# Four RMS norms moved into the stages that produce their input, and two plain fp32 slices at the start of three output projections

## The reference, cut to what matters

```python
def rms_norm(x, g):
    xf = x.astype(jnp.float32)
    y = xf * lax.rsqrt(jnp.mean(xf * xf, axis=-1, keepdims=True) + EPS)
    return (y * g.astype(jnp.float32)).astype(x.dtype)

x = x + jnp.concatenate([y_a, y_b, y_m], axis=-1) @ w_out   # even layer; the odd layer has the same form
```

## Time and profile before

| | |
|---|---|
| median of 3 runs | 2514.02 us (2512.58 to 2516.36) |
| the profiled execution's own time | 2516.36 us |
| its span on the core | 2515.1 us |
| PE busy | 2372.6 us (94%) |
| DVE busy | 1924.6 us (77%) |
| ACT busy | 1162.9 us (46%) |
| mean granted TensorE clock | 0.971 of full speed |
| `even_out` | 194 to 232 us |
| `odd_out` | 430 to 470 us |
| LRU block | 480 to 582 us |
| `mla_out` | 1584 to 1618 us |

### The profile page before, as it was taken

One profiled execution on the slowest core, in us unless ns is written; L12 is line 12 of the kernel. 1 busy time (PEld: TensorE's weight loads), 2 busy tenths in 40 slices (PEclk: granted clock), 3 DMA queues, 4 the chain that ended last, 5 costly groups with the idle time before them and its releaser, 6 DMA issues. The chain is left out here.

```text
span 2515.1 us, 37964 instructions
## 1 busy us (share of the span) xinstructions
PE 2372.6 (94%) x11691; PEld 1939.4 (77%) x11691; DVE 1924.6 (77%) x4365; ACT 1162.9 (46%) x2015; POOL 153.2 (6%) x170
## 2 busy tenths in 40 slices
PE   7998989898998999999999989899899999999997
PEld 5775457675886888888888856678778888888886
DVE  5676677765998788888888855589977777777776
ACT  5674245341177544444444434414854444444443
POOL 0000000000253000000000000013500000000000
PEclk9998988998999999999999989899999999999999
DMA  7523640564112676777767751212055555555553
GB/s 259 186 89 127 232 169 1 179 231 143 59 51 71 209 254 251 261 255 247 257 249 259 257 182 68 84 59 85 26 177 195 188 189 194 185 195 188 191 193 134
DMA packets 144614, 429.30 MB, mean 171 GB/s; under 512 B 15231, under 2 KB 21375, under 8 KB 144511
## 3 DMA queue, kind: packets, MB, share of 16 engines
q1 hardware_dynamic: 144510, 428.08, 48.7%
HBM read 426.99 MB, written 1.05 MB: 170 GB/s over the span
## 5 line engine op out<-in xcount | busy, mean ns | idle before, releaser
L3241 PE MATMUL bank<-h_t_parts,u_t_high 128*128 128x512 f32 x1824 | 450.5, 389 | 0.0
L3241 PEld LDWEIGHTS bank<-h_t_parts,u_t_high 128*128 128x128 f32 x1824 | 342.5, 188 | 71.0
L3325 ACT ACTIVATE u_t_high<-u_ring 128x1024 fp32r<-128x1024 f32 x228 | 242.0, 1061 | 184.3 <-DMA u_ring<-in_peer_u 182.3
L3344 ACT ACTIVATE activated<-activated 128x256 f32<-128x256 f32 x228 | 95.7, 420 | 472.5 <-DVE activated L3394 472.5
L3255 PE MATMUL bank<-v_high,weighted_high 128*128 128x512 f32 x976 | 306.2, 395 | 5.4 <-DVE weighted_low L3406 5.4
L3381 DVE TENSOR_TENSOR u_t_low<-u_ring,u_t_high 128x1024 fp32r<-128x1024 f32 x228 | 278.8, 1223 | 40.5 <-ACT u_t_high L3325 28.9
L3255 PE MATMUL bank<-v_low,weighted_high 128*128 128x512 f32 x976 | 303.9, 392 | 0.0
L3255 PE MATMUL bank<-v_high,weighted_low 128*128 128x512 f32 x976 | 302.5, 391 | 0.0
L3388 DVE TENSOR_TENSOR v_low<-v_ring,v_high 128x1024 fp32r<-128x1024 f32 x244 | 296.9, 1217 | 6.0 <-ACT v_high L3332 3.3
L3332 ACT ACTIVATE v_high<-v_ring 128x1024 fp32r<-128x1024 f32 x244 | 257.1, 1054 | 49.6 <-PE bank L3255 48.1
L3244 PEld LDWEIGHTS bank<-h_t_parts,u_t_low 128*128 128x128 f32 x1824 | 248.9, 190 | 17.7
(11 more groups left out here) (588 smaller groups left out, 3682.1 us busy)
## 6 DMA issues: line engine op xcount, KB each, us to landing
v_ring<-in_peer_v SPq DMA_DIRECT2D x244, 512.0 KB, 3.4
u_ring<-in_peer_u SPq DMA_DIRECT2D x228, 512.0 KB, 4.6
panel<-in_l_w_in SPq DMA_DIRECT2D x15, 2048.0 KB, 8.0
late_tiles<-in_ada_w SPq DMA_DIRECT2D x54, 512.0 KB, 4.3
mod_ring<-in_ada_w SPq DMA_DIRECT2D x42, 512.0 KB, 4.6
panel<-in_peer_w_q SPq DMA_DIRECT2D x8, 2048.0 KB, 7.8
panel<-in_l_w_out SPq DMA_DIRECT2D x4, 2560.0 KB, 8.9
early_u<-in_peer_u SPq DMA_DIRECT2D x20, 512.0 KB, 3.4
```

The source lines that it names most:

```text
L3241: nc.tensor.matmul(banks[2 + k][:, :], UTH[:, k, j, :], H2[:, j, :, :].rearrange("p a s -> p (a s)"), start=(j == 0), stop=False, skip_gro ...
L3325: nc.scalar.activation(UTH[:, s, :, :].rearrange("p a b -> p (a b)"), UR[:, s, :], ACT.Copy)\
L3344: nc.scalar.activation(AA[:, s, :], AA[:, s, :], ACT.Gelu).then_inc(gelued, 1)
```

## The change

It touches nothing but the four places and what lies between them.

- `project_rows` takes `plain=2`: the first two slices of the first panel are one plain fp32 product per row tile, of the panel as it was loaded and a plain fp32 copy `SP` of the turned source (ACT, into a tile of its own). Their weights are not split in panel 0. `SH` of these slices is still made by ACT in turn, `SL` by DVE from `SP` and `SH` behind `w_low` of the last slice of panel 0, since panel 1 needs them.
- Three turns come first, and `turn(m + 3)` stands behind slice m, instead of two and `turn(m + 2)`.
- `half_squares`: the norm's squares are summed by halves of 512 columns as `X` is finished: ACT does (panel 0, both row tiles) behind `w_high` of slice 5 of panel 1 and (panel 1, row tile 0) at the end, each into a PSUM bank that nobody reads; DVE does (panel 1, row tile 1), and adds the two sums.
- The rest of the norm (`normed_turned`, unchanged) follows in the same stage, in the three projections and in the LRU block. Four norm stages go.
- The two gain stages become `gain_work`, DVE work ahead of the last results in `odd_out` and in the LRU block. Two stages go.

```diff
@@ project_rows @@
+        xn = nc.alloc_sbuf_tensor_at(f"rows_normed{n}", [P, NT, D], F32, offset=zone.at)
...
+        x_done = [sem(f"rows{n}_x_done{x}") for x in range(4)]
+        squares_act, squares_dve = half_squares([banks[4], banks[5]])
+        end_act, end_dve, end_pe = normed_turned(X, xn, jobs)
...
+        SP = zone("plain_rows", [P, plain, S]) if plain else None
...
             def _(pe):
                 def turn(m):
-                    if m >= 4:
-                        pe.wait_ge(src_low, m - 3)
+                    if m - 4 >= plain:
+                        pe.wait_ge(src_low, m - 3 - plain)
+                    elif m >= 4:
+                        pe.wait_ge(src_high, m - 3)
...
-                turn(0)
-                turn(1)
+                for m in range(3):
+                    turn(m)
...
-                    if i == 0:
-                        pe.wait_ge(src_low, m + 1)
-                    pe.wait_ge(w_low, q + 1)
-                    high, low = ring[:, q % 4, 0, :], ring[:, q % 4, 1, :]
+                    if q < plain:
+                        pe.wait_ge(src_plain, m + 1)
+                        if m == 0:
+                            wait_panel(pe, ps[i])
+                        products = ((SP, weights(q)),)
+                    else:
+                        n = nth[q]
+                        if i == 0:
+                            pe.wait_ge(src_low, m + 1 - plain)
+                        elif i == 1 and m < plain:
+                            pe.wait_ge(src_low, K - plain + m + 1)
+                        pe.wait_ge(w_low, n + 1)
+                        high, low = ring[:, n % 4, 0, :], ring[:, n % 4, 1, :]
+                        products = ((SH, high), (SH, low), (SL, high))
...
-                    if i == 0 and m + 2 < K:
-                        turn(m + 2)
+                    if i == 0 and m + 3 < K:
+                        turn(m + 3)
+                end_pe(pe)
...
             def _(act):
...
                     if i == 0:
                         act.wait_ge(turned, m + 1)
+                        if m < plain:
+                            nc.scalar.activation(SP[:, m, :], banks[4 + m % 4][:, 0:S], ACT.Copy).then_inc(src_plain, 1)
                         nc.scalar.activation(SH[:, m, :], banks[4 + m % 4][:, 0:S], ACT.Copy).then_inc(src_high, 1)
...
+                    if i == 1 and m == 5:
+                        for t in range(NT):
+                            x_there(act, 0, t)
+                            squares_act(f, act, 0, t)
                 sqrt_table()
+                x_there(act, 1, 0)
+                squares_act(f, act, 1, 0)
+                end_act(f, act)
...
             def _(dve):
...
+                    if i == 0 and m == K - 1:
+                        for x in range(plain):
+                            nc.vector.tensor_tensor(SL[:, x, :], SP[:, x, :], SH[:, x, :].bitcast(F32), ALU.subtract)\
+                                .then_inc(src_low, 1)
                     if m == 2 and i > 0:
                         evacuate(f, dve, i - 1)
                     modulation.add(f, dve, plan[q])
+                if gains:
+                    gains(f)
                 evacuate(f, dve, len(ps) - 1)
+                x_there(dve, 1, 1)
+                squares_dve(f, dve, xn[:, 1, 512:1024])
+                end_dve(f, dve)
@@ new @@
+    def half_squares(junk):
+        sq = sem(f"norm{Stage.count}_half_squares")
+        cell = lambda i, t: stats[:, 60 + 2 * i + t:61 + 2 * i + t]
+        half = lambda i, t: X[:, t, i * 512:(i + 1) * 512]
+
+        def on_act(f, act, i, t):
+            if i:
+                act.wait_ge(sq, t + 1)
+            f(nc.scalar.activation(junk[t][:, :], half(i, t), ACT.Square, accum_out=cell(i, t)), sq, wait=False)
+
+        def on_dve(f, dve, own):
+            f(nc.vector.scalar_tensor_tensor(own, half(1, 1), 1.0, half(1, 1), ALU.mult, ALU.mult, accum_out=cell(1, 1)))
+            dve.wait_ge(sq, 3)
+            f(nc.vector.tensor_tensor(stats[:, 0:2], stats[:, 60:62], stats[:, 62:64], ALU.add))
+        return on_act, on_dve
@@ lru_block, on DVE @@
+                gain_work([(1, sc2, C("norm_ffn_g_2", 0, 8))], 24, 40)(f)
                 dve.wait_ge(row_stored, 2)
...
+                squares_dve(f, dve, xn[:, 1, 512:1024])
+                end_dve(f, dve)
@@ callers @@
-    norm_transpose(X, HT, [(HT, C("l1_norm", 0, 8), None)])
...
-    gain_stage([(0, sc1, C("norm_mix_g_2", 0, 8))], 0, 16)
-    norm_transpose(X, HT, [(HT, GM[:, 0, :], sh1)])
...
-    def peer(l, q_name, gain, shift, gate_cols, jobs=None, gains=None):
-        norm_transpose(X, HT, [(HT, gain, shift)])
+    def peer(l, q_name, gate_cols, jobs=None, gains=None):
...
-    gain_stage([(1, sc2, C("norm_ffn_g_2", 0, 8))], 24, 40)
```

More of the change, by code:

```diff
@@ L521, in project_split, with project_rows @@
         zone.at = mark
-    def project_rows(name, rows, order, evac, ready=None, at_act=None, at_dve=None, at_pe=None, mod_steps=(0, 0)):
+    def project_rows(name, rows, order, evac, jobs, gains=None, gated=False, ready=None, at_act=None, at_dve=None,
+                     at_pe=None, mod_steps=(0, 0), plain=0):
         if not stage():
@@ L546, in weights, with wait_used @@
             return slots[ps[i] % 3][:, order[m] * 512:(order[m] + 1) * 512]
-        def wait_used(eng, q):
-            i, m = slices[q]
+        split_of = slices[plain:]
+        nth = {q: q - plain for q in range(plain, len(slices))}
+        def wait_used(eng, n):
+            i, m = split_of[n]
             if m == K - 1:
@@ L558, in evacuate, with x_there @@
                 dve.wait_ge(acc_ready, g + 1)
-                evac(f, "v", i, t, acc_bank(g), acc_free["v"])
+                evac(f, "v", i, t, acc_bank(g), acc_free["v"], x_done[2 * i + t])
+        def x_there(eng, i, t):
+            if gated:
+                eng.wait_ge(x_done[2 * i + t], 1)
+            else:
+                eng.wait_ge(acc_free["v"], owners[:g0 + 2 * i + t + 1].count("v"))
         with StageBlock() as block:
@@ L624, in _ @@
                         at_dve[q](f, dve)
-                    if i == 0:
+                    if i == 0 and m >= plain:
                         dve.wait_ge(src_high, m + 1)
@@ L2396, in build, with mods, gain_work, work @@
     attention(units, score_banks=(0, 1, 6), beside=dict(pe=cmp_att_pe, act=cmp_att_act, dve=cmp_att_dve))
+    def mods(base):
+        return [MOD[:, base + 8 * i:base + 8 * i + 8] for i in range(6)]
+    def gain_work(jobs, a, b):
+        def work(f):
+            f(nc.vector.tensor_tensor(MOD[:, a:b], MOD[:, a:b], C("ada_b_2", a, b - a), ALU.add))
+            for i, scale, gain in jobs:
+                f(nc.vector.scalar_tensor_tensor(GM[:, i, :], scale, 1.0, gain, ALU.add, ALU.mult), wait=False)
+        return work
+    sh1, sc1, g1, sh2, sc2, g2 = mods(0)
     def odd_output():
@@ L2408, in odd_output @@
         zone.at = odd_mix_end
-        project_rows("odd_out", lambda k, t: mix[:, t, k * P:(k + 1) * P], MIX_ORDER, add_to_x(),
-                     ready={4: (rows_m, 1), 6: (rows_d, 1)}, at_dve={1: dve_memory, 2: dve_gated}, mod_steps=(6, 10))
+        project_rows("odd_out", lambda k, t: mix[:, t, k * P:(k + 1) * P], MIX_ORDER, add_to_x(), [(HT, GM[:, 0, :], sh1)],
+                     gains=gain_work([(0, sc1, C("norm_mix_g_2", 0, 8))], 0, 16), ready={4: (rows_m, 1), 6: (rows_d, 1)}, at_dve={1: dve_memory, 2: dve_gated}, mod_steps=(6, 10), plain=2)
     odd_output()
     zone.at = WORK
-    def mods(base):
-        return [MOD[:, base + 8 * i:base + 8 * i + 8] for i in range(6)]
-    def gain_stage(jobs, a, b):
-        def body(f, dve):
-            f(nc.vector.tensor_tensor(MOD[:, a:b], MOD[:, a:b], C("ada_b_2", a, b - a), ALU.add))
-            for i, scale, gain in jobs:
-                f(nc.vector.scalar_tensor_tensor(GM[:, i, :], scale, 1.0, gain, ALU.add, ALU.mult), wait=False)
-        elementwise(body)
     def gate_row(cols, unbiased=None):
@@ L2501, in lru_block @@
         halves = [slice(0, KD // 2), slice(KD // 2, KD)]
+        x_done = [sem(f"lru_x_done{x}") for x in range(4)]
+        xn = zone("normed", [P, NT, D])
+        squares_act, squares_dve = half_squares([banks[4], banks[5]])
+        end_act, end_dve, end_pe = normed_turned(X, xn, [(HT, GM[:, 1, :], sh2)])
         with StageBlock() as block:
@@ L2618, in _ @@
                 sqrt_table()
+                f = act_f.on(act)
+                for i, t in ((0, 0), (0, 1), (1, 0)):
+                    act.wait_ge(x_done[2 * i + t], 1)
+                    squares_act(f, act, i, t)
+                end_act(f, act)
             @block.vector
```

57 lines of the change are left out of this document (33 added, 24 removed).

## The result

| | before | changed |
|---|---|---|
| median | 2514.34 us (4 runs, 2512.58 to 2516.36) | 2491.27 us (4 runs, 2489.9 to 2492.93) |
| the profiled execution | 2516.36 us, span 2515.1 | 2489.9 us, span 2488.7 |
| mean granted clock | 0.971 | 0.980 |
| ratio | | 0.9907 [0.9896, 0.9919] |

The changed kernel is 23.1 us faster by the medians and 26.4 us by the two profiled spans. The profile before is that of the slowest of its four executions, the profile of the changed kernel that of its fastest, so the two traces overstate the difference by 3.3 us.

A forecast was written before the change was run, and what follows sets the result against it. In the four short places it took chains between PE, DVE and ACT as the bound, not a full engine; 5.0 + 2.3 + 1.75 + 5.35 = 14.4 us took 2514.02 to 2499.6 us, range 2494.5 to 2506.

The forecast's parts named there:

- the half-clock stretches behind each of the four norms: Behind the four norms: an unknown of the sum, some 3 us shorter or longer, either sign, 1.7 us for each.
- First panels: Panel 0 of the three projections: 5.0 us less in `odd_out`, 2.3 in `even_out`, 1.75 in `mla_out`.
- The step for `even_out`'s turn 6: `even_out` panel 0: PE reaches turn 6 behind slice 3 and stands 2.1 us for DVE's gated rows.
- The deferred pair in `mla_out`: Two deferred `src_low` on DVE, 0.8 us both, delay panel 1's fourth slice: ready at 1606.7, wanted at 1606.0.
- Panel 1 I leave at its length: `odd_out` panel 1: length unchanged, since DVE still waits 1.50 us there for a modulation tile.
- Tails: Last addition to mean, three projections and LRU block: each becomes 0.97 us, saving 0.84, 1.63, 2.03 and 0.85, 5.35 us together.
- ACT's half square into PSUM: At the norms: ACT's write into PSUM, not in the trace, fits even at twice a copy, 1.3 us.
- Rival 1: Half clock stays at the three starts, costing 1.7 us in each block: 2504.7 us; chance 0.22.
- Rival 2: PE's queue still waits for DVE and ACT; panels 0 gain nothing, only tails count: 2508.7 us; chance 0.11.
- Rival 3: Slower: plain passes do not bring the clock back in panel 0; about 2546 us; chance 0.03.
- Rival 4: The split norm brings nothing and tails keep their length: 9.1 us gained, 2504.9 us; chance 0.04.
- The rule set against the forecast: At block starts: transposes don't count as busy for the clock gate, so the six there are a rest of PE.

The follow-up runs named there:

- e6: The changed kernel with a DVE-only delay stage of four additions (4.1 us) ahead of `even_out`; 2502.45 us, ratio 0.9945.
- e8: The kernel before with six unread plain products at the start of each of its four separate norm stages; 2501.68 us, ratio 0.9950.
- e7: The changed kernel with eight unread plain products behind the last product of each of the four blocks; 2485.57 us, ratio 0.9883.
- e11: e7 with turn 6 of `even_out` put behind slice 4 instead of slice 3; 2484.20 us, ratio 0.9882.
- e9: e1 with the unread products added in the norms; 2497.32 us, ratio 0.9926.
- e1: The changed kernel without plain slices and with two turns first instead of three, so norms and gains moved only; 2506.49 us, ratio 0.9959.
- e2: The changed kernel without plain slices, keeping the moved norms and three turns first; 2499.25 us, ratio 0.9941.
- e10: e2 with the unread products added in the norms; 2494.37 us, ratio 0.9915.
- e5: The changed kernel with a DVE-only delay stage of one addition (1.9 us) ahead of `even_out`; 2494.19 us, ratio 0.9912.

## Why the prediction was wrong

**The step that failed most** is the one put last under the sum: "the half-clock stretches behind each of the four norms may come out some 3 us shorter or longer ... which is either sign and 1.7 us for each". I took that term as zero. It measured 8.3 us between the two profiled executions and 5.2 by the medians. In the traces it is 2.2 us behind `even_out`, 2.2 behind `odd_out`, 1.7 behind the LRU block, nothing behind `mla_out` (10.2 us both times), and 2.1 in the latent input, behind a fifth norm that the prediction did not list. The three that moved became 6.8 us shorter and not 3; the time for each was near all the same, since a microsecond of half clock costs some 0.3 us there and not half. That they would all go one way was not seen, and the zero in the middle was wrong: the kernel before had 44 us of them, where kernels with moved norms have 32 on average, which by that price is some 4 us. The rest is, as far as the runs show, luck: 24 us in place of 32. e6 shows that a shift in timing moves them, and e8 that they cost the kernel before 12.6 us.

**First panels.** Forecast 5.0 us for `odd_out`, 2.3 for `even_out` and 1.75 for `mla_out`. From first turn to the first product of panel 1 it became 5.2, 3.2 and, for `mla_out`, 3.4 less 0.5 in panel 1: 2.3 us more than the 9.05. For `even_out` and `mla_out` the forecast ended panel 0 at the start of its last product (216.76 and 1604.4 us), 0.2 us early in each. The larger error is one price: a turn was counted as 0.38 us, and adds 0.25 between slices. With seven, seven and five turns behind slices that is 0.9, 0.9 and 0.65 us too much. In `odd_out` most of it was used up by the start, 1.08 us in place of 0.9, and by waits of PE that the forecast took as gone, 0.31 us of them at the first product of panel 1. The step for `even_out`'s turn 6 held: 2.1 us of waiting forecast, 1.71 measured, on the same instruction. The deferred pair in `mla_out` took 0.76 us as counted, but lengthened panel 1 by 0.5 us, not 0.7.

**"Panel 1 I leave at its length"** failed: from its first product to the end of the last addition 16.71 became 15.56 us, since the tile that DVE waited 1.50 us for was there. With filled norms the wait is back (1.07 us in e7, 1.29 in e11) and panel 1 takes 16.27 and 16.49 us, so this 1.1 us is not safely a gain of the change.

**Tails.** 0.97 us from last addition to mean was forecast; 0.97 to 1.03 was measured. 5.35 us for the norms: PE's time from a block's last product to the norm's first transpose fell by 0.83, 1.68, 2.11 and 0.84 us in the changed kernel, 5.5 in all, and e9 has 4.4 to 6.0. This term was right. ACT's half square into PSUM, bounded at 1.3 us, takes 0.60.

**Rivals.** Rival 1 (the half clock stays at the three starts) is false for the changed kernel but true without plain slices: e1, e2, e9 and e10 all have it at `even_out` and `mla_out`, e1 and e9 at `odd_out` too. With the kernels before and e8 it is 16 of 18 starts without plain slices. With them it is 1 of 22 (`odd_out` in e11), leaving out `even_out` in e5 and e6, where the delay stands ahead of it. Rival 2 (the waits only move) is refuted by the places of e10; only turn 6 is such a wait. Rival 3 is refuted by the clock of 1.00 in all first panels. Rival 4 is refuted by the tails and by e9. The rule set against the forecast, that transposes are a rest as far as the clock goes, held for the row it came from, but not in general: in twelve of the 32 stretches the clock rose with nothing behind PE's rest but 16 transposes.

With the clock of the norms held up in both kernels, the change is worth 16.1 us by the medians, against 14.4 forecast. By that reading the other 7 of the 23.1 us are the clock behind the norms; the own pieces (17.9 us) put it at 5.2.

## What to carry to other kernels

Ahead of a forecast, list every stretch at half clock, in the code that the change doesn't touch too, and ask whether they stand at the long or the short end of what such rests give; the expected shift is not zero at either end. Look also at which executions the two traces are of. Where PE rests some 5 us behind dense work, as in these norms, products that nobody reads keep the clock up: here they brought 12.6 us to one kernel and 5 to 7 to the other. Count them so that they do not outlast the rest. That they make the times of other edits steadier isn't shown: executions spread by 3.2 to 6.7 us with filled norms and by 2.5 to 12.9 without. Compare edits by the lengths of their own places, cut at fixed instructions, and let the total only confirm. Count an instruction squeezed between others by what it adds to the distance of its neighbours, not by its own duration.

## What the runs showed of the hardware that was not expected

- The same rest of 4.48 us ahead of the same 16 transposes is followed by 3.4 us at half clock in one kernel and by 10.2 us in another whose only edit is a delay of 4.1 us, some 270 us earlier (changed and e6). What differs is where the clock falls: 0.48 us ahead of the first transpose in one, 0.78 us in the other. In a norm that PE rests through, most transposes take 417 to 421 ns; in the filled norms they take 273.
- Products of 384 columns with nothing to compute cost nothing beyond their time: eight take 5.32 us. Behind `even_out` the transposes then begin 5.39 us behind the start of the last product, and 4.92 us in the changed kernel, so seven products would have been nearer there (an estimate).
- Transposes alone can be followed by a rise of the clock: behind `odd_out` in the changed kernel it rose at 464.23 us, with 14 of the 16 transposes begun and no product since the rest. The Trainium skill says in TensorE: Matmul & The Clock Gate, section Part 4: PE-mode transpose, that transposes don't count as busy for the gate. The kernel before agrees behind `even_out` (clock 0.50 to their end), but twelve of the 32 stretches do not, and the measurement decides.
- A plain fp32 turn of two transposes lasts 0.38 us in the trace and costs 0.25 us between products.
